# Odd layer: values as three fp32r products of split probabilities and values, with the output gate's columns ahead of the values in each block

## The reference, cut to what matters

```python
q, k, v, o, z, gates = split(h @ w_in)            # v, o, z: 2048 columns each
q, k = silu(dw_conv(q, k))
# mlstm_chunkwise, forward and backward, in steps of 64 tokens:
#   s   = (q k^T) * exp(decay - m_row)
#   num = s v + w_prev * (C q);  den = sum(s) + w_prev * (n q)
#   h   = num / max(|den|, exp(-m_row))
h = (h_f + h_b) * sigmoid(o)
h = rms_norm(h per head, head_norm)
y_lat = (h * silu(z)) @ w_out
```

## Time and profile before

| | |
|---|---|
| median of 3 runs | 1780.7 us (1780.66 to 1781.59) |
| profiled execution | 1779.69 us, of which the span is 1777.9 us |
| granted TensorE clock | 0.997 of full |
| PE busy | 1726.9 us, 97% |
| DVE busy | 1171.6 us, 66% |
| ACT busy | 917.4 us, 52% |
| odd layer's blocks and heads | about 628 to 905 us |

### The profile page before, as it was taken

One profiled execution on the slowest core, in us unless ns is written; L12 is line 12 of the kernel. 1 busy time (PEld: TensorE's weight loads), 2 busy tenths in 40 slices (PEclk: granted clock), 3 DMA queues, 4 the chain that ended last, 5 costly groups with the idle time before them and its releaser, 6 DMA issues. The chain is left out here.

```text
span 1777.9 us, 22905 instructions
## 1 busy us (share of the span) xinstructions
PE 1726.9 (97%) x8559; PEld 1394.2 (78%) x8559; DVE 1171.6 (66%) x2154; ACT 917.4 (52%) x1497; POOL 49.5 (3%) x68
## 2 busy tenths in 40 slices
PE   8999999999998999999999999999999999999998
PEld 3776788777787777777778787788887787878886
DVE  6654576688437567666867775777646867577744
ACT  4333554333336356655656556467534756547743
POOL 0000000000000000000100002000000002000000
PEclk9999999999999999999999999999999999999999
DMA  9456221211425444443444444555555454555562
GB/s 331 158 200 226 96 69 51 72 59 60 142 95 188 129 124 138 148 149 104 172 156 150 142 154 163 171 179 193 195 189 158 133 169 141 182 165 180 191 217 74
DMA packets 115974, 267.25 MB, mean 150 GB/s; under 512 B 5412, under 2 KB 9837, under 8 KB 115672
## 3 DMA queue, kind: packets, MB, share of 16 engines
q1 hardware_dynamic: 111384, 252.26, 43.4%
q0 software_dynamic: 3504, 10.96, 2.0%
q10 hardware_dynamic: 976, 2.57, 0.4%
HBM read 264.63 MB, written 1.14 MB: 149 GB/s over the span
## 5 line engine op out<-in xcount | busy, mean ns | idle before, releaser
L155 DVE TENSOR_TENSOR qw_rest<-weights,qw_lead 128x1024 fp32r<-128x1024 f32 (+2 forms) x428 | 520.2, 1222 | 378.9 <-ACT qw_lead L343 373.4
L343 ACT ACTIVATE qw_lead<-weights 128x1024 fp32r<-128x1024 f32 (+2 forms) x428 | 446.4, 1048 | 459.6 <-PE psum L182 420.6
L182 PE MATMUL psum<-qw_lead,b_h_pair 128*128 128x512 f32 (+1 forms) x960 | 319.8, 398 | 4.1 <-ACT b_gates L2991 1.3
L182 PEld LDWEIGHTS psum<-qw_lead,b_h_pair 128*128 128x128 f32 x960 | 180.3, 188 | 44.7 <-issue 3.7
L182 PE MATMUL psum<-qw_rest,b_h_pair 128*128 128x512 f32 (+1 forms) x480 | 186.2, 388 | 0.0
L175 PE MATMUL psum<-b_h_pair,qw_lead 128*128 128x512 f32 x512 | 178.1, 393 | 2.0 <-DVE b_h_pair L722 2.0
L176 PE MATMUL psum<-b_h_pair,qw_rest 128*128 128x256 f32 x512 | 142.6, 279 | 0.0
L182 PE MATMUL psum<-e_h_lead,qw_lead 128*128 128x512 f32 x320 | 132.2, 413 | 2.2 <-DVE e_qT L1588 1.5
L182 PE MATMUL psum<-e_h_lead,qw_rest 128*128 128x512 f32 x320 | 125.8, 393 | 0.0
L182 PE MATMUL psum<-e_h_rest,qw_lead 128*128 128x512 f32 x320 | 125.3, 391 | 0.0
L175 PEld LDWEIGHTS psum<-b_h_pair,qw_lead 128*128 128x128 f32 x512 | 95.9, 187 | 24.4 <-DVE b_h_pair L722 2.9
(11 more groups left out here) (490 smaller groups left out, 3036.6 us busy)
## 6 DMA issues: line engine op xcount, KB each, us to landing
weights<-in_w_in SPq DMA_DIRECT2D x48, 1024.0 KB, 5.1
weights<-in_o_w_in SPq DMA_DIRECT2D x32, 1024.0 KB, 5.4
weights<-in_w_mlp_up SPq DMA_DIRECT2D x32, 1024.0 KB, 5.6
weights<-in_w_mlp_down SPq DMA_DIRECT2D x32, 1024.0 KB, 4.9
weights<-in_e_w_in SPq DMA_DIRECT2D x26, 1024.0 KB, 5.1
weights<-in_w_mod SPq DMA_DIRECT2D x24, 1024.0 KB, 7.1
weights<-in_e_w_out SPq DMA_DIRECT2D x8, 1024.0 KB, 5.0
weights<-in_o_w_out SPq DMA_DIRECT2D x8, 1024.0 KB, 4.8
```

The source lines that it names most:

```text
L155: return eng.tensor_tensor(self.rest[at], src, self.lead[at].bitcast(F32), ALU.subtract)
L182: mm = nc.tensor.matmul(out, l, r, start=start and i == 0, stop=stop and i == 2)
L343: self.core.nc.scalar.activation(self.buf.lead[self.at(u)], self.raw(u), ACT.Copy).then_inc(self.lead_ready, 1)
```

## The change

- Probabilities and values are split. `WT` becomes one lead and one rest of 128x512 (before: two fp32 buffers, one per tile), `v` one lead and one rest of 128x4x512 (before: two fp32 buffers, one per block in turn). The value product of a tile is 4 chunks x 3 fp32r products.
- A new DVE program `prob_rests` at s+4.05 subtracts the lead from PSUM. `copies` now waits for the previous tile's values from the second tile on. All four v tiles are read by ACT (lead) and then by DVE (rest). The first lead of a block's values waits until the previous pair's values are done.
- In each block o takes the places 0 to 4, v 4 to 12, z stays at 12 to 16. The weight stream has the same order.
- `values` move from s+4.3 to s+4.5, `outs` from s+4.7 to s+4.9, `squares` from s+5.0 to s+5.2.
- The turned result's lead lies where the keys were and its rest in the place of the o gate; the wait of the first four turns for values is dropped.

```diff
--- before.py
+++ after.py
@@ -250,7 +250,7 @@
     cols("o_k", w, (OD_K,))
     cols("o_k2", w, (OD_K + 512,))
     for i in range(4):
-        for name, lo in (("o_v", OD_V), ("o_o", OD_O), ("o_z", OD_Z)):
+        for name, lo in (("o_o", OD_O), ("o_v", OD_V), ("o_z", OD_Z)):
             cols(f"{name}{i}", w, (lo + i * BANK,))
     rows("o_out", a["o_w_out"][0])
     for l in range(DEPTH):
@@ -2209,19 +2209,18 @@
 class HeadFeatures:
 
 
-    def __init__(self, split, first):
-        self.split, self.first = split, first
+    def __init__(self, lead, rest):
+        self.leads, self.rests = lead, rest
 
     def lead(self, n):
-        return self.split.lead[:, 2 * n:2 * n + 2, :].rearrange("p k t -> p (k t)")
+        return self.leads[:, 2 * n:2 * n + 2, :].rearrange("p k t -> p (k t)")
 
     def rest(self, n):
-        z = self.first if n < 4 else self.split.rest
-        return z[:, 2 * n:2 * n + 2, :].rearrange("p k t -> p (k t)")
+        return self.rests[:, :, n * ML_V:(n + 1) * ML_V]
 
     def parts(self, at):
-        lead, rest = self.split.parts(at)
-        return lead, self.first[at] if at[1] < 8 else rest
+        _, k, part = at
+        return self.leads[at], self.rests[:, k % 2, k // 2 * ML_V + part.start:k // 2 * ML_V + part.stop]
 
 
 class OddRoom:
@@ -2229,22 +2228,23 @@
         nc = core.nc
         sb = lambda s, name, shape: s.enter_context(nc.sbuf_tensor("o_" + name, shape, F32))
         with ExitStack() as c:
-            v1 = sb(c, "v1", [P, NT, 2 * ML_V])
             with ExitStack() as early:
-                self.v = (sb(early, "v0", [P, NT, 2 * ML_V]), v1)
+                self.v = Split(nc, early, "o_v", [P, NT, 2 * ML_V])
                 self.kT = sb(early, "kT", [P, ML_H, 2 * SEQ])
                 self.h = Split(nc, early, "o_h", [P, KC, 2 * SEQ])
+                with ExitStack() as turned:
+                    hs_rest = turned.enter_context(nc.sbuf_tensor("o_hs_rest", [P, LT, ML_H * ML_V], F32R))
                 self.o_gate = sb(early, "o", [P, LT, ML_H * ML_V])
                 with ExitStack() as gates:
                     self.wg = Split(nc, gates, "o_wg", [P, KC, P])
                 self.Dm = sb(early, "decay", [P, LT, 2, 2 * SEQ])
-                self.WT = sb(early, "WT", [P, LT, 2 * SEQ])
+                self.WT = Split(nc, early, "o_WT", [P, 2 * SEQ])
                 self.spread = sb(early, "spread", [P, 2, 2 * SEQ])
-            hs_first = c.enter_context(nc.sbuf_tensor("o_hs_first", [P, 8, SEQ], F32R))
-            self.hsT = Split(nc, c, "o_hsT", [P, 16, SEQ])
+            sb(c, "under_hsT", [P, 2, NT, 2 * ML_V])
+            hs_lead = c.enter_context(nc.sbuf_tensor("o_hs_lead", [P, 16, SEQ], F32R))
         flat = core.hT[:].rearrange("p k t -> p (k t)")
         self.z = flat[:, 0:2048].rearrange("p (i t n) -> p i t n", i=2, t=LT)
-        self.out_src = HeadFeatures(self.hsT, hs_first)
+        self.out_src = HeadFeatures(hs_lead, hs_rest)
         self.gain = flat[:, 2048:3072].rearrange("p (i n) -> p i n", i=2)
         self.scratch, self.wg32 = flat[0:40, 0:3072].rearrange("p (n t) -> p n t", n=6), flat[:, 3072:3712]
         self.junk = flat[:, 3712:3968]
@@ -2397,7 +2397,7 @@
         self.negmax, self.decayed, self.floored, self.scored = s("negmax"), s("decayed"), s("floored"), s("scored")
         self.mixed, self.turned, self.WT_ready, self.valued, self.out_done, self.squared = s("mixed"), s("turned"), s("WT_ready"), s("valued"), s("out_done"), s("squared")
         self.tensor = (self.scores, self.turns, self.values)
-        self.vector, self.scalar, self.gpsimd = (self.maxima, self.mixes, self.outs), (self.decays, self.copies, self.squares), (self.spreads,)
+        self.vector, self.scalar, self.gpsimd = (self.maxima, self.mixes, self.prob_rests, self.outs), (self.decays, self.copies, self.squares), (self.spreads,)
 
     def logs(self):
 
@@ -2495,34 +2495,40 @@
         for j, h, t, at in self.jobs(3.9):
             yield at
             act.wait_ge(self.turned, j + 1)
-            if j >= LT:
-                act.wait_ge(self.valued, j - 1)
-            self.core.nc.scalar.activation(self.odd.WT[:, t, :], self.core.ps[:, self.banks[2], :], ACT.Copy).then_inc(self.WT_ready, 1)
+            if j:
+                act.wait_ge(self.valued, j)
+            self.core.nc.scalar.activation(self.odd.WT.lead[:], self.core.ps[:, self.banks[2], :], ACT.Copy).then_inc(self.WT_ready, 1)
+
+    def prob_rests(self, dve):
+        for j, h, t, at in self.jobs(4.05):
+            yield at
+            dve.wait_ge(self.WT_ready, 2 * j + 1)
+            self.odd.WT.take_rest(self.core.nc.vector, np.s_[:], self.core.ps[:, self.banks[2], :]).then_inc(self.WT_ready, 1)
 
     def values(self, pe):
         nc, ps, odd = self.core.nc, self.core.ps, self.odd
-        for j, h, t, at in self.jobs(4.3):
+        for j, h, t, at in self.jobs(4.5):
             yield at
             if t == 0 and h % 2 == 0:
-                self.dense.wait_first(pe, 8 * (h // 2) + 4)
-            pe.wait_ge(self.WT_ready, j + 1)
+                self.dense.wait_first(pe, 8 * (h // 2) + 6)
+            pe.wait_ge(self.WT_ready, 2 * j + 2)
             for b in range(4):
-                mm = nc.tensor.matmul(ps[:, self.banks[2], 0:ML_V], odd.WT[:, t, b * P:(b + 1) * P], odd.v[h // 2 % 2][:, b, pair_of(h)], start=(b == 0), stop=(b == 3))
+                mm = split_matmul(nc, ps[:, self.banks[2], 0:ML_V], odd.WT.parts(np.s_[:, b * P:(b + 1) * P]), odd.v.parts((slice(None), b, pair_of(h))), b == 0, b == 3)
             mm.then_inc(self.valued, 1)
 
     def outs(self, dve):
         odd = self.odd
-        for j, h, t, at in self.jobs(4.7):
+        for j, h, t, at in self.jobs(4.9):
             yield at
             if t == 0 and h % 2 == 0:
-                self.dense.wait_first(dve, 8 * (h // 2) + 6)
+                self.dense.wait_first(dve, 8 * (h // 2) + 2)
             dve.wait_ge(self.valued, j + 1)
             z = odd.o_gate[:, t, h * ML_V:(h + 1) * ML_V]
             self.core.nc.vector.tensor_tensor(z, self.core.ps[:, self.banks[2], 0:ML_V], z, ALU.mult).then_inc(self.out_done, 1)
 
     def squares(self, act):
         odd = self.odd
-        for j, h, t, at in self.jobs(5.0):
+        for j, h, t, at in self.jobs(5.2):
             yield at
             act.wait_ge(self.out_done, j + 1)
             if j:
@@ -2597,13 +2603,12 @@
     starts = [11.7 + 16 * (h // 2) + 6.0 * (h % 2) for h in range(ML_H)]
     taps_done = core.sem("taps_done")
 
-    def v_out(i, g):
-        def free(eng):
-            if i >= 2 and g < 2:
-                eng.wait_ge(heads.valued, 4 * (i - 1))
-        act = lambda act, src: (free(act), nc.scalar.activation(odd.v[i % 2][:, g, :], src, ACT.Copy))[1]
-        dve = lambda dve, src: (free(dve), nc.vector.tensor_copy(odd.v[i % 2][:, g, :], src))[1]
-        return dict(act=act) if g % 2 == 0 else dict(dve=dve)
+    def v_lead(i, g):
+        def out(act, src):
+            if i and g == 0:
+                act.wait_ge(heads.valued, 4 * i)
+            return nc.scalar.activation(odd.v.lead[:, g, :], src, ACT.Copy)
+        return out
 
     def z_out(i, g):
         def out(act, src):
@@ -2614,12 +2619,12 @@
     items = []
     for i in range(4):
         at, cs = 16.0 * i, slice(i * BANK, (i + 1) * BANK)
+        u = first[f"o_o{i}"]
+        items.append(Item(**span(range(u, u + 4), at, 1.0), groups=tokens(LT), src=odd.h,
+                          act=lambda g, cs=cs: lambda act, src: nc.scalar.activation(odd.o_gate[:, g, cs], src, ACT.Sigmoid)))
         u = first[f"o_v{i}"]
-        items.append(Item(**span(range(u, u + 4), at, 2.0), groups=tokens(NT), src=odd.h,
-                          act=lambda g, i=i: v_out(i, g).get("act"), dve=lambda g, i=i: v_out(i, g).get("dve")))
-        u = first[f"o_o{i}"]
-        items.append(Item(**span(range(u, u + 4), at + 8, 1.0), groups=tokens(LT), src=odd.h,
-                          act=lambda g, cs=cs: lambda act, src: nc.scalar.activation(odd.o_gate[:, g, cs], src, ACT.Sigmoid)))
+        items.append(Item(**span(range(u, u + 4), at + 4, 2.0), groups=tokens(NT), src=odd.h, act=lambda g, i=i: v_lead(i, g),
+                          dve=lambda g: lambda dve, src: odd.v.take_rest(nc.vector, np.s_[:, g, :], src)))
         u = first[f"o_z{i}"]
         items.append(Item(**span(range(u, u + 4), at + 12, 1.0), groups=tokens(LT), src=odd.h, act=lambda g, i=i: z_out(i, g)))
     dense = Dense(core, "o_in_", items, (0, 1, 2, 3))
@@ -2641,8 +2646,6 @@
 
     def turn_ready(pe, n):
         pe.wait_ge(norm.scaled, 2 * n + 2)
-        if n < 4:
-            pe.wait_ge(heads.valued, 12)
     turn = Turn(core, "od_t_", blocks, [57.0, 58.2, 59.4, 60.6, 63.2, 63.9, 70.0, 76.0], (5,),
                 act=lambda n: lambda act, src: nc.scalar.activation(hsT.lead(n), src, ACT.Copy),
                 dve=lambda n: lambda dve, src: nc.vector.tensor_tensor(hsT.rest(n), src, hsT.lead(n).bitcast(F32), ALU.subtract),
```

## The result

The change makes the kernel slower. The changed kernel takes 1787.57 us (median of 7 runs, 1784.15 to 1789.58), the kernel before 1781.59 us on the same chip (1780.66 to 1782.89): ratio 1.0037, 95% interval 1.0028 to 1.0047. A second set of runs beside the experiments gave 1.0046 (1.0033 to 1.0058). The forecast was 1778.1 us; the range ended at 1785.5.

A forecast was written before the change was run, and what follows sets the result against it. PE, busy 97% of the span, was taken to bound the kernel. Terms -4.6 + 2.1 - 1.4 + 1.3 = -2.6 us took 1779.69 to 1777.1; the median, 1.0 above, gave 1778.1 us, range 1773.5 to 1785.5.

The forecast's parts named there:

- (d): Other value tiles, single v buffer, z's bank, weight order and block 0's gates: all covered, at no cost.
- (a): Head B's first tile, three times: PE stalls at turn and values behind DVE and ACT; +2.1 us, bounds 0 to 4.5.
- R3: Rival, 12%: o first starves the layer's start or the v stream; PE waits for weights in block 0, 1 to 4 us.
- (b): Head A's first tile, four times: ACT's weight lead comes some 0.4 us earlier, so PE waits less for DVE's mix; -1.4 us.
- (c): Where the output projection begins, once: head 4's rest stands behind the new probabilities' rest in DVE's list; +1.3 us.
- The products: Value products on PE, 16 tiles: twelve fp32r products take 1.44 us a tile instead of 1.73; -4.6 us.
- R2: Rival, 17%: DVE becomes the bound between places 16 and 24 of each block; 1784.1 us if 2 us later, 1787 at 3.
- R4: Rival, 3%: each switch of ACT's tables costs the drain too; some +18 us, giving 1796 us.

The follow-up runs named there:

- five banks: Changed kernel with a fifth PSUM bank in the dense projection's turn, against the kernel before: ratio 1.0014.
- order alone: Kernel before with only the columns' order changed to o, v, z, values and probabilities still fp32, against the kernel before: ratio 1.0038.
- fp32 products: Changed kernel with four fp32 products of the leads per tile, rests made but not multiplied, against the kernel before: ratio 1.0055.
- rest first: Changed kernel with the probabilities' rest at s+4.15 instead of s+4.05, behind head 4's result rest, against the kernel before: ratio 1.0024.
- Sigmoids together: Changed kernel with Sigmoids moved behind head B's last Exp (blocks 1 to 3) and ahead of the gates' Exp (block 0), against the kernel before: 1.0007.
- mix earlier: Changed kernel with fifth bank, moved Sigmoids, head 4's rest ahead, and two weight rests per block made later, against the kernel before: ratio 0.9950.

## Why the prediction was wrong, step by step

- **The step that failed is in (d), "At no cost".** It followed the banks for one tile only ("z's bank waits for v's first rest: 1.5 places") and not for the others. The fourth v tile has 1.4 places from the o tile's Sigmoid in its bank to its first product. The walk of (a) had the very numbers: ACT's second Sigmoid ends at about 758.0, and PE turns B's first tile at 756.7 and reaches the fourth v tile at 757.1 (0.36 later, as in the kernel before: 757.26 and 757.62). Its 1.0 us wait could be read off; I looked only for what waits for the copy at the end of that list. It costs 5.8 us in four waits (3.06, 1.01, 1.02 and 0.70), shown by five banks and by the Sigmoids' places, each of which takes 4 to 5 us of it away.
- **R3 had the place and not the mechanism.** In block 0 PE waits 3.1 us at the start of the v stream, which R3 priced at 1 to 4 us; but it waits for a Sigmoid, not for weights. (d) had looked at the gates' Exp in block 0 for what waits for the gates, and not for the second Sigmoid that now stands behind it. From 640 to 905 us no wait for a weight rest over 0.2 us shows in the changed kernel.
- **The low clock was in no term.** Every one of the five profiles with a wait of 3.05 us in block 0 has the clock at 1.2 GHz behind it (changed twice, order alone, fp32 products, rest first), and none of the others. Every one with a wait of 2.1 at head 5 has it there (changed twice, fp32 products, five banks, Sigmoids together), and none with 0.9 to 1.1. In the changed kernel each costs 1.7 us, 3.4 in all. Removing either wait took its low clock away (experiments 3, 4 and 5). That a wait of this length always does it is not shown: elsewhere in these traces it does not (last section).
- **(a) was right in the lists and hidden in the sum.** ACT has just the seven table loads more (four at the Sigmoid, three at the Exp), B's turn waits 0.16 once, and the value product's 0.6 appears with five banks. In the changed kernel it adds nothing (2.1 us forecast), because it lies behind the wait for the Sigmoid.
- **(b) did not come.** Forecast -1.4; head A's four waits are 0.97, 0.60, 0.70 and 0.30 us against 0.74, 0.74, 0.75 and 0.22 before, +0.1 in all, and with B's 0.16 the row grows from 2.4 to 2.7. Order alone removes the wait altogether. In block 2 the Exp's table load stands 1.38 us ahead of head A's score with the order alone (786.71 against 788.09), 0.90 in the changed kernel (787.34 against 788.24) and 0.76 before (782.23 against 782.99). The difference is the fourth v tile: ACT copies it in the changed kernel (0.58) right ahead of the table load, while with fp32 values DVE copies it. I counted that copy, but put the weight lead ahead of it at 780.3, 2.7 us ahead of the score; it stands 2.46 ahead (785.78 against 788.24; 780.67 against 782.99, or 2.32, before), so most of the 0.4 I expected was not there. In block 0 the lead is later still (671.71 against 673.89, 2.18), and there the wait grew. That the copy is the reason is read from the lists and was not tried by itself.
- **(c) was right:** +1.2 measured, 1.3 forecast, and the clock on top.
- **The products were right:** 1.44 us a tile; 3.7 to 4.3 us by the stretches, 4.6 forecast with 3.8 to 5.4 as bounds.

The account of the stretch, changed less before: waits for o tiles +5.8, mix +0.3, head 5's turn +1.2, low clock +3.4, products -4.0 (middle of 3.7 and 4.3): +6.7. Measured: 283.7 - 276.6 = +7.1. Some 0.4 us stays unaccounted. The range failed since its high end was built on R2, a DVE that is late three times; PE was late through ACT and a bank. (R2's sum reads 2.6 + 3 x 2 = +3.4; the 2.6 should have its minus sign, and the times it gives are right.)

R4 did not come about. Seven table loads more would have cost ACT about 2.66 us each by the Trainium skill, "ScalarE: Activation LUTs", section "What ACT_TABLE_LOAD costs"; the trace does not agree: load at 757.90, Exp at 759.19, 1.29 us.

## What to carry to other kernels

When the order of work on the bounding engine changes, write down for every tile which buffer it takes, who read that buffer last, and how many places lie between; do it for each tile and not for one. Where a list of another engine has been walked through, ask of every instruction in it, not only of the last, who waits for it. A wait on TensorE can cost more than its length: here the clock fell behind waits of 3.05 and 2.14 us, and each fall cost another 1.7. A change that is right on the bounding engine can be saved without touching its arithmetic: a fifth bank and new places for the Sigmoids and for three rests turned 1.0037 into 0.9950.

## What was not expected of the hardware

- In the stretch the granted clock fell to 0.50 (1.2 GHz) behind single waits as short as 2.14 us, each time for about 3.4 us (twice that with the order alone), and never behind single waits of 1.1 us or less. Outside it the length of the wait does not decide. At 564 to 566 us, where nothing was changed, PE waits 2.89 us in the kernel with head 4's rest first and the clock falls; it waits 2.96 us in the one with the mix earlier and the clock stays. At the start of the next layer all 13 profiles have waits of 1.1 and 0.6 us close behind each other, and the clock falls behind them in seven; at 1337 to 1354 us all have a wait of 2.00 us, and it falls in five. What else decides is open.
- Such falls come at 562, 920 and 1350 us in the changed kernel and at 34 and 358 us in the kernel before (one more stands at the end of every profile). The one at 562 lasts twice as long, windows 562 to 570. Runs of one kernel spread over 2 to 7 us, up to four times the 1.7 us that one such stretch costs; whether the number of them makes the whole spread was not tried.
- With the order alone the clock stayed low twice as long in block 0 behind the same wait of 3.05 us: the windows from 648 to 656 have 0.69, 0.50, 0.50 and 0.61. It fell while PE still stood (PE starts at 649.70), so of the 3.4 us of shortfall about 2.9 count. In the changed kernel it fell after PE had started (651.26; window 650 to 652 has 0.96). Why it lasts twice as long is open.
- An fp32 product of 256 columns costs 0.43 us against 0.12 for one fp32r product, a factor of 3.6. The Trainium skill, "FP8 and Floating Point Precision", section "TensorE Precision Notes", has four passes for fp32; the trace is near that.
